# Latent attention of a two-block layer: rotated scores in passes of four 32-row tiles, scores of two steps together

## What is computed

```python
def mla_attend(qn, qr, kn, kr, v):
    s = (jnp.einsum('bqhd,bkhd->bhqk', qn, kn, preferred_element_type=jnp.float32)
         + jnp.einsum('bqhr,bkr->bhqk', qr, kr, preferred_element_type=jnp.float32)) * MLA_SCALE
    p = jax.nn.softmax(s, axis=-1)
    o = jnp.einsum('bhqk,bkhd->bqhd', p.astype(v.dtype), v)
    return o.reshape(qn.shape[0], qn.shape[1], H_B * V_B)
```

## Time and profile before

| | us |
|---|---|
| median of 3 runs | 638.72 (637.94 to 639.18) |
| the profiled execution | 637.48 |
| its span, first to last instruction | 635.7 |
| TensorE matmuls busy | 575.6 (91%) |
| VectorE busy | 294.7 (46%) |
| ScalarE busy | 216.8 (34%) |
| GpSimd busy | 38.9 (6%) |
| mean DMA rate | 304 GB/s |

### The profile page before, as it was taken

One profiled execution on the slowest core, in us unless ns is written; L12 is line 12 of the kernel. 1 busy time (PEld: TensorE's weight loads), 2 busy tenths in 40 slices (PEclk: granted clock), 3 DMA queues, 4 the chain that ended last, 5 costly groups with the idle time before them and its releaser, 6 DMA issues.

```text
span 635.7 us, 8825 instructions
## 1 busy us (share of the span) xinstructions
PE 575.6 (91%) x3506; PEld 373.9 (59%) x3506; DVE 294.7 (46%) x697; ACT 216.8 (34%) x462; POOL 38.9 (6%) x68
## 2 busy tenths in 40 slices
PE   7999999999999999999998999999989876766785
PEld 7898977787867887878773444445353421311232
DVE  3355377765668978674737767125220100100002
ACT  4344444644533622665327745022110100100002
POOL 2000000000000000010003434000000000000000
PEclk9999999999999999999999999999999986879888
DMA  8594974659679877526696233668999999999994
GB/s 354 172 403 161 377 312 182 239 228 401 275 289 433 335 285 263 213 103 236 245 375 273 92 101 133 245 252 325 407 428 426 429 428 426 427 423 433 425 418 195
DMA packets 22925, 193.36 MB, mean 304 GB/s; under 512 B 4194, under 2 KB 5602, under 8 KB 11236
## 3 DMA queue, kind: packets, MB, share of 16 engines
q1 hardware_dynamic: 19140, 189.28, 74.4%
q10 hardware_dynamic: 3456, 1.94, 1.1%
q0 software_dynamic: 288, 1.57, 0.6%
HBM read 191.21 MB, written 1.06 MB: 302 GB/s over the span
## 4 chain that ended last, share of the span: by engine, by line
PE 62%; DMA 22%; DVE 7%; ACT 3%; SPq 3%; issue 2%; POOL 1%; ACTq 0%; POOLq 0%; DVEq 0%
PE bank L1242 24%; DMA ring<-in_stream 20%; PE bank L1884 5%; PE bank L1219 5%; PE bank L1230 5%; SPq L819 2%; PE bank L1820 2%; PE bank L1290 2%; PE bank L1748 2%; PE bank L1683 2%; PE bank L1806 2%; PE bank L1535 2%; PE bank L1930 1%; DMA vvc<-vvc 1%; PE bank L1642 1%
## 5 line engine op out<-in xcount | busy, mean ns | idle before, releaser
L1242 PE MATMUL bank<-weight_parts,u_parts 128*128 128x512 f32 (+1 forms) x384 | 116.6, 386 | 0.8 <-DVE weight_parts L2199 0.4
L2199 DVE TENSOR_TENSOR weight_parts<-ring,weight_parts 128x1024 fp32r<-128x1024 f32 (+1 forms) x60 | 69.4, 1190 | 35.7 <-ACT weight_parts L845 33.7
L1242 PEld LDWEIGHTS bank<-weight_parts,u_parts 128*128 128x128 f32 x384 | 69.9, 188 | 17.1 <-issue 1.8
L845 ACT ACTIVATE weight_parts<-ring 128x1024 fp32r<-128x1024 f32 (+1 forms) x60 | 59.9, 1029 | 32.6 <-PE bank L1242 19.9
L1242 PE MATMUL bank<-weight_parts,x_parts 128*128 128x512 f32 (+1 forms) x128 | 48.4, 378 | 0.0
L1242 PE MATMUL bank<-u_parts,weight_parts 128*128 128x256 f32 x192 | 36.5, 286 | 1.3 <-issue 0.6
L1195 POOL TENSOR_TENSOR small<-small 128x1 f32<-128x1 f32 (+1 forms) x14 | 8.5, 611 | 414.4 <-DVE small L2617 198.3
L912 ACT ACTIVATE sp<-sp,small 128x128 f32<-128x128 f32 (+1 forms) x48 | 21.3, 444 | 32.6 <-DVE small L2108 32.6
L1242 PEld LDWEIGHTS bank<-u_parts,weight_parts 128*128 128x128 f32 x192 | 30.4, 191 | 2.8 <-issue 1.6
L1143 ACT ACTIVATE sp<-bank 128x512 f32<-128x512 f32 x4 | 2.4, 598 | 75.5 <-PE bank L1884 75.5
L1242 PE MATMUL bank<-x_parts,weight_parts 128*128 128x256 f32 x96 | 27.1, 283 | 0.0
(11 more groups left out here) (363 smaller groups left out, 1060.0 us busy)
## 6 DMA issues: line engine op xcount, KB each, us to landing
ring<-in_stream SPq DMA_DIRECT2D x37, 2048.0 KB, 9.1
qk<-in_stream SPq DMA_DIRECT2D x9, 2048.0 KB, 12.1
parts<-in_stream SPq DMA_DIRECT2D x9, 2048.0 KB, 19.5
tabs<-in_stream SPq DMA_DIRECT2D x5, 2048.0 KB, 23.3
mo<-in_stream SPq DMA_DIRECT2D x5, 2048.0 KB, 26.4
vvc<-in_stream SPq DMA_DIRECT2D x5, 2048.0 KB, 29.6
vvc<-in_vecs SPq DMA_DIRECT2D x12, 512.0 KB, 8.5
parts<-in_stream SPq DMA_DIRECT2D x6, 1024.0 KB, 34.1
```

The source lines that it names most:

```text
L845: ins = act.activation(dst, src, ACT.Copy, scale=scale)
L1242: ins = pe_.matmul(o, lhs(a, c, i), rhs(b, c, i), start=(c == 0 and n == 0), stop=(c == chunks - 1 and n == 2))
L2199: dve.tensor_tensor(quarter(low, name, q), quarter(slot(name), name, q), quarter(high, name, q).bitcast(F32), ALU.subtract).then_inc(split ...
```

## The change

It touches four places.

1. TensorE: at an even step `latent_scores` first multiplies the rotated part of all four units of the head pair, in four tiles of 32 rows (rows 0, 64, 32, 96 or the other way round) into the four score banks. The unrotated passes follow at each step, add to the banks and complete them. Only an even step waits for the banks, for all four units before.
2. TensorE's loop: the scores of even step s+1 move from the head of step s to its end, for s = 7, 9, 11 and 13. Those of odd steps stay at the head.
3. ScalarE: the rotated queries are copied in two pieces, so that the heads of a pair lie on the right rows after the transpose for both halves of the queries.
4. VectorE: in an even latent step it takes the maxima of the next step's units as well, and does its copy of a transposed unit behind them.

```diff
--- before.py
+++ after.py
@@ -1057,7 +1057,11 @@
                         if h == 0:
                             copy(qnT[:, 2 * t:2 * t + 2, :], D_(name)[:, :].rearrange("p (j s) -> p j s", j=2), name)
                         else:
-                            copy(qrow[:, t, :, :], D_(name)[:, 0:HB * ROPE].rearrange("p (h d) -> p h d", h=HB), name)
+                            src, dst = (x.rearrange("p (a i d) -> p a i d", a=HB // 2, i=2)
+                                        for x in (D_(name)[:, 0:HB * ROPE], qrow[:, t, :, :].rearrange("p h d -> p (h d)")))
+                            for i in range(2):
+                                ins = copy(dst[:, :, i], src[:, :, (i + t) % 2])
+                            leave(ins, name)
                     elif name[:3] in ("ckv", "xkv"):
 
                         filled(eng, name)
@@ -1549,10 +1553,12 @@
                 if s == 2:
                     for x in [x for x in DENSE if x not in ROUTER][-2:]:
                         kept(eng, x)
-                if s >= 3:
+                if s in range(3, 8):
                     eng.wait_ge(u_masked, 2 * s - 2)
+                if s == 8:
+                    eng.wait_ge(u_masked, 2 * s)
                 if s >= 10:
-                    eng.wait_ge(u_exp, 2 * s - 2)
+                    eng.wait_ge(u_exp, 2 * s)
 
             def window_scores(s):
 
@@ -1634,18 +1640,19 @@
                 if s == 8:
                     for x in ("qr", "kr"):
                         kept(eng, x)
-                scores_free(s)
                 j, _, q = unit_of(2 * s)
-                cols = slice(q * P, (q + 1) * P)
+                if q == 0:
+                    scores_free(s)
+                    for i in range(TOK):
+                        for b in range(2):
+                            a = HD * b + ROPE * ((i + j) % 2)
+                            h = slice(a, a + ROPE)
+                            pe_.matmul(score_bank(2 * s + 2 * i + b)[:, :], qrT[h, j // 2, i * P:(i + 1) * P], krT[h, :],
+                                       start=True, stop=False, tile_position=(a, 0))
                 for b in range(2):
                     h = slice(HD * b, HD * b + HD)
-                    pe_.matmul(score_bank(2 * s + b)[:, :], qnT[h, j, cols], knT[h, j, :], start=True, stop=False,
-                               tile_position=(HD * b, 0))
-                for b in range(2):
-                    a = HD * b + ROPE * (j % 2)
-                    h = slice(a, a + ROPE)
-                    pe_.matmul(score_bank(2 * s + b)[:, :], qrT[h, j // 2, cols], krT[h, :], start=False, stop=True,
-                               tile_position=(a, 0)).then_inc(u_scores, 1)
+                    pe_.matmul(score_bank(2 * s + b)[:, :], qnT[h, j, q * P:(q + 1) * P], knT[h, j, :], start=False, stop=True,
+                               tile_position=(HD * b, 0)).then_inc(u_scores, 1)
 
             def unit_turn(u):
                 if u >= 16 and u % 2 == 0:
@@ -1828,7 +1835,7 @@
                 for ahead in (2, 3) if s == 2 else (s + 1,):
                     if ahead < 8:
                         window_scores(ahead)
-                    elif ahead < 16:
+                    elif ahead < 16 and ahead % 2:
                         latent_scores(ahead)
                 if s >= 3:
                     first_tile = 0 if s % 2 else 2
@@ -1837,6 +1844,8 @@
                     first_output(0, 0, 4)
                 unit_turn(2 * s - 2)
                 unit_turn(2 * s - 1)
+                if s in (7, 9, 11, 13):
+                    latent_scores(s + 1)
             first_output(0, 4, 6)
             pair_pv(7, range(4))
             first_output(1, 0, 6)
@@ -2451,18 +2460,38 @@
                         kept(eng, name)
                         dve.tensor_tensor(wr, wr, bc(scl[:, 2, :], 32), ALU.mult).then_inc(wr_scaled, 1)
 
+            def vector_turned(u):
+
+                if vector_turns(u):
+                    unit_turned(eng, u, dve.tensor_copy).then_inc(u_turned_v, 1)
+
             for s in range(2, 17):
-                if s < 16:
+                if s < 8:
                     for u in (2 * s, 2 * s + 1):
                         unit_max(u)
                         unit_neg(u)
-                        if 3 <= u - 2 < 16:
+                        if u - 2 >= 3:
                             unit_scale(u - 2)
-                if 8 <= s < 16:
+                    vector_turned(2 * s - 1)
+                elif s == 16:
+                    vector_turned(2 * s - 1)
+                elif s % 2 == 0:
+                    for u in (2 * s, 2 * s + 1):
+                        unit_max(u)
+                        unit_neg(u)
+                        if u - 2 < 16:
+                            unit_scale(u - 2)
                     unit_recip(2 * s)
-                if vector_turns(2 * s - 1):
-                    unit_turned(eng, 2 * s - 1, dve.tensor_copy).then_inc(u_turned_v, 1)
-                if 8 <= s < 16:
+                    unit_max(2 * s + 2)
+                    unit_neg(2 * s + 2)
+                    unit_recip(2 * s + 1)
+                    unit_scale(2 * s + 1)
+                    unit_max(2 * s + 3)
+                    unit_neg(2 * s + 3)
+                    vector_turned(2 * s - 1)
+                else:
+                    unit_recip(2 * s)
+                    vector_turned(2 * s - 1)
                     unit_recip(2 * s + 1)
                     unit_scale(2 * s + 1)
```

## The result

The changed kernel takes 644.6 us (median of four runs, 642.82 to 648.52) against 638.67 for the kernel before in the same session. The ratio is 1.0094, 95% interval 1.0067 to 1.0121. A second set of six runs gave 646.31 (643.7 to 648.63), ratio 1.0103 [1.0082, 1.0124]. The ten runs together have a median of 645.3. The change costs 5.9 us in the first set and 7.4 in the second, and its ten runs lie 5.8 us apart.

What follows compares the result with a forecast made beforehand. Bound: engines, with TensorE dense in the latent stage, then the expert-weight stream, lateness passing one for one. Stalls of 8.88 net less 4.22 of passes gave +4.7 us: 643.4 against 638.72, range 641.3 to 646.0.

Steps and rivals of the forecast that it cites:

- The stalls: Latent stage: TensorE waits before values and transposes, mainly for VectorE's late copy; 9.71 us, 8.88 net of the old gap.
- The passes: Latent stage, TensorE: four of eight rotated passes go, at 1.055 us each, saving 4.2 us.
- the pair that I put at 9.05: Latent stage: a steady head pair, rotated pass to next rotated pass, takes 9.05 us against 8.3.
- One for one to the end: Latent stage to end: TensorE's lateness moves the saturated weight stream and the end by as much, +4.7 us.
- I charge nothing: TensorE's granted clock in the latent stage: at 80% busy it stays at 2.4 GHz, so no cost.
- ScalarE's copy alone: Rival: value products wait only for ScalarE's copy, stalls shrink to 4.2 us, 0.8 us faster, 637.9; chance 5%.
- Two by two: Rival: the four row tiles of a rotated pass run two at a time, +8.9 us, 647.6; chance 5%.
- Absorbed: Rival: the last, transfer-paced part absorbs the lateness; full absorption gives 638.7 us, half 641; chance 5%.
- worth its 4.2 us: Rival: VectorE catches up and nothing stalls in the latent stage, so 634.5 us; chance 2%.
- The two-piece copy: Rotated queries leave PSUM in two copies, perhaps 0.25 us each, under ScalarE idle time; no cost.
- The new wait on the exponentials: A pair's first rotated pass waits for the previous pair's last exponential, which is long over; no cost.

Runs made afterwards that it cites:

- Kernels 5: The changed kernel with 14 unread identity transposes on TensorE in each of the four long gaps before value products: 643.18 us, ratio 1.0064.
- kernel 6: The kernel before the change with the unrotated pass of each even latent step done twice, a delay without new gaps: 642.9 us, ratio 1.0072.
- Kernel 2: The changed kernel with VectorE's copy moved ahead of the fourth maximum, and the second unit's scaling behind it: 638.53 us, ratio 0.9989.
- kernel 9: The changed kernel with rotated passes on two row tiles, not four, and 14 unread transposes in each of the four long gaps: 647.59 us, ratio 1.0119.
- kernel 4: The changed kernel rearranged: first latent pair as before, later values' second half behind the next transposes, VectorE's copy before the fourth maximum: 636.38 us, ratio 0.9958.
- kernel 8: The kernel before the change with only the two-piece copy of the rotated queries and its row layout: 638.8 us, ratio 0.9995.
- kernel 7: The changed kernel with VectorE's copy and scaling back ahead of the third and fourth maximum: 640.98 us, ratio 1.0036.
- kernel 3: The changed kernel with the rotated matmuls on two row tiles in place of four: 649.93 us, ratio 1.0167.
- kernel 10: The rearranged kernel (values' second half as cover, VectorE's copy earlier) with two row tiles in its three joint rotated passes: 639.42 us, ratio 1.0005.

## Why the prediction was right, and where it was not

The forecast was 643.4 us, slower, in a range of 641.3 to 646.0; 644.6 was measured. That it lies inside the range is partly luck of the draw: the median of the second set, 646.31, is outside, and so are four of the ten runs. For the profiled execution the forecast was 642.2, and 642.8 was measured. By its steps:

- **The stalls.** They were named in place, number and cause, and the sum held. From start to start (the idle times in brackets are shorter, because modelled ends reach into them), forecast and measured: before 360.32, 0.90 and 0.89 (1.92 less 1.03 of transposes); before 361.53, 0.24 and 0.19; before 362.78, 0.74 and 0.76; the first pair, 0.09 + 2.37 and 2.60; three more pairs, 1.79 and 1.96 each. Together 9.71 forecast and 10.32 measured. The 1.96 is 377.04 to 380.03 (2.99) less 1.03.
- **The passes.** I took 1.055 for every pass. The joint rotated pass took 1.07, which was right. But a pass behind one of the same tile shape is cheaper: both unrotated passes together 1.92. A pair's scores went from 4.22 to 2.99 us, 1.23 less rather than 1.055. Four times: 4.92 saved, not 4.22. Stalls 10.32 less the old one of 0.89 less 4.92 is +4.5, and the stage shows +4.53. Two errors of 0.6 to 0.7 us cancelled, and the pair that I put at 9.05 took 9.03.
- **One for one to the end.** The stage lost 4.5, the experts began 5.0 later (0.5 of it from ahead of the stage), the span grew by 5.3. From the last pair's values to the first experts it is 38.2 us in eleven of the thirteen profiles, before and after the change alike. Kernels 5 and 6 say the same: +4.5 gives +4.3, +3.4 gives +4.0. The lateness was not absorbed.
- **The step that was mis-sized is the clock: "I charge nothing".** My reason was a stretch of the expert part with 7.52 us of work in 10 at a granted clock of 1.00. That row was one stretch of one execution, chosen without a fall: the row above it in the same group has 141.33 busy of 180.10 us, 78%, at a mean of 0.89. The changed kernel's stage ran at 1.00 throughout in one profile and fell to the lower level three times in the other, which cost 4.8 us. Filling the gaps left the stage as it was and brought the median to 643.18, within 0.3 of the forecast. The term that I left out is therefore 645.3 less 643.2, about 2 us in the median, 0 to 5 in a single run. Kernel 2 gives the same size: its stage, at 1.00 throughout, is 4.5 us shorter than the change's at 1.00, and its median 6.8 below 645.3. That the fill works through the clock is inferred: the profiles are two of the change and one of the fill.
- **The rivals.** *ScalarE's copy alone*: fell with the gap of 1.90, which ends 0.10 after VectorE's copy, and with kernel 2. *Two by two*: fell with the pass of 1.07 us against 1.91 in kernel 9. *Absorbed* and *worth its 4.2 us* fell with the result; of the second's 4.2 us kernel 4 reached 2.5, 0.85 from the tiles in each of three pairs, once the order let them.
- **Costs put at nothing.** The two-piece copy: nothing (kernel 8). The new wait on the exponentials: nothing in the change, where the last unit's exponential starts at 379.35 and takes 0.69, 2 us ahead of the pass at 382.07; 0.82 in each pair as soon as VectorE's copy went first (kernel 7). In the change it was covered by the longer stall.

The rule weighed in the prediction (the Trainium skill, "TensorE: Matmul & The Clock Gate", Part 3, packing: 3.07 times the rate for four row tiles) would have made the four-tile pass an estimated 1.38 us. Here four float32 tiles took 1.07 us where two took 1.05, so the measurement decides: the third and fourth tile add 0.02 us.

## What to carry to other kernels

Before scores, or any other work, are merged into one place, ask what they covered where they stood: here two passes hid the copies of transposed tiles, and the merge laid bare 10 us of waits to save 5. The saving came only when other work (the values' second half) took over the cover and VectorE's copy was put between the third and fourth maximum, and then it was 2.5 us. On an engine that is late for two consumers, list its instructions with both due times and place each one by them. And a gap in a stage that was dense can be dearer than its length, as the two profiles of the change show: price it once at its length and once with the clock down behind it, and put the second in the range.

## What the hardware showed that I had not expected

- **The clock can fall behind gaps of about 2 us, in some executions and not in others.** In the execution of 648.63 us it was at 1.2 GHz in three places, each 0.2 to 1.1 us behind the end of a gap of 1.9 to 2.2 us; products of values then took 1.37 from start to start against 1.01, four transposes 0.91 to 0.99 against 0.50, a rotated pass 1.41 against 1.07. With two tiles (kernel 3) it fell inside the gap and stayed down for over 12 us. With useless transposes in the gaps it was at 1.00 in the stage of both kernels that had them (5 and 9, one profile each), and the runs spread by 1.6 and 2.3 us, against 5.8 and 5.1 without them (the change's ten runs and kernel 3's four). The Trainium skill ("TensorE: Matmul & The Clock Gate", Part 4) says of transposes that the clock gate does not count them as work in the same way; no number here bears that out: in these two kernels float32 transposes, which the profile records as MATMUL with the identity, were the whole filling. Nor does a fall need a long gap: one came 2.1 us behind a gap of 0.82 us (kernel 10), and the profiles of kernels 2 and 8 have one in the router, with 0.57 from 432 to 436 us, where TensorE stood idle nowhere just before; there it cost 1.2 us on the way to the experts. What decides between one execution and the next stays open.
- **Two passes of one tile shape, one behind the other, cost 0.2 us less than two apart.** A repeated unrotated pass adds 0.86 (kernel 6), the second of two in the change 0.86 (1.92 less 1.06), a second round of two 32-row tiles 0.85 (kernel 9), against 1.05 to 1.07 for a pass between others. The saving is not all in the second pass: in kernel 6 both take 0.96 from start to start (360.09, 361.05, 362.01). The Trainium skill ("TensorEngine Tiling (Array Packing)", Key Properties) says that a change of tiling mode drains the engine; the 0.2 us are in line with it, but no run here takes it apart from other causes.
